# Both weight buffers of a decoder step moved by 64 bytes in the on-chip memory

## The reference

```
proj  = einsum('btnc,ncd->btnd', br, w_branch)
x = x + sum(sigmoid(zg) * proj) @ w_o
h = rmsnorm(x) @ w_up
x = x + square(relu(h)) @ w_down
```

## Time and profile before

| | |
|---|---|
| median of 3 runs | 943.7 us (943.46 to 943.88) |
| profiled execution | 943.61 us, its span 941.8 us |
| TensorE matmuls | 937.0 us busy, 7930 instructions |
| TensorE weight loads | 907.2 us busy, 7930 instructions |
| VectorE | 671.2 us busy |
| ScalarE | 476.8 us busy |
| GpSimd | 40.9 us busy |
| granted TensorE clock | 1.000 of full speed |

### The profile page before, as it was taken

The page is one execution under the profiler, slowest core; times in us unless marked ns, Lnnn a source line. Parts: engine busy times, 40 slices in busy tenths (PEclk is TensorE's granted clock), DMA queues, the critical chain, the costliest instruction groups (busy, mean ns, idle before and its releaser), DMA issues.

```text
span 941.8 us, 18907 instructions
## 1 busy us (share of the span) xinstructions
PE 937.0 (99%) x7930; PEld 907.2 (96%) x7930; DVE 671.2 (71%) x1057; ACT 476.8 (51%) x708; POOL 40.9 (4%) x61
## 2 busy tenths in 40 slices
PE   9999999999999999999999999999999999999998
PEld 8999898999999999999999998999999999999998
DVE  7788788948866765555758787889498676656464
ACT  7439553463654353534653586436537543535261
POOL 0340000000000000000004200000000000000000
PEclk9999999999999999999999999999999999999999
DMA  8756444444454585454557453544444546645542
GB/s 314 261 197 207 151 147 135 136 138 154 157 180 138 198 300 188 159 180 151 174 178 265 167 218 110 168 129 142 136 151 158 169 149 222 202 158 163 187 144 95
DMA packets 44853, 164.26 MB, mean 174 GB/s; under 512 B 5057, under 2 KB 7489, under 8 KB 44225
## 3 DMA queue, kind: packets, MB, share of 16 engines
q1 hardware_dynamic: 43488, 153.03, 48.6%
q0 software_dynamic: 1136, 9.83, 2.7%
q10 hardware_dynamic: 144, 0.20, 0.1%
HBM read 153.30 MB, written 10.29 MB: 174 GB/s over the span
## 4 chain that ended last, share of the span: by engine, by line
PE 98%; DMA 1%; ACT 0%; SPq 0%; DVE 0%; issue 0%; ACTq 0%
PE pz L440 90%; PE pm L440 6%; DMA xp<-in_x_in 1%; PE pm L635 1%; DVE w_lo L1083 0%; ACT w_hi L852 0%; PE pm L698 0%; PE pm L688 0%; SPq L381 0%; SPq L383 0%; ACT rstd L870 0%; ACT w_hi L1031 0%; PE pm L587 0%; ACT a_hi L861 0%; DVE xp L1128 0%
## 5 line engine op out<-in xcount | busy, mean ns | idle before, releaser
L852 ACT ACTIVATE w_hi<-raw 128x1024 fp32r<-128x1024 f32 x265 | 274.1, 1050 | 199.4 <-PE pz L440 194.7
L440 PE MATMUL pz<-a_hi,w_hi 128*128 128x288 f32 x1376 | 370.7, 300 | 0.9 <-ACT w_hi L1031 0.5
L440 PE MATMUL pz<-a_hi,w_lo 128*128 128x288 f32 x1376 | 364.8, 295 | 0.0
L440 PE MATMUL pz<-a_lo,w_hi 128*128 128x288 f32 x1376 | 363.5, 294 | 0.0
L1083 DVE TENSOR_TENSOR w_lo<-raw,w_hi 128x1024 fp32r<-128x1024 f32 x265 | 321.0, 1221 | 37.4 <-ACT w_hi L852 37.3
L440 PEld LDWEIGHTS pz<-a_hi,w_hi 128*128 128x128 f32 x1376 | 244.9, 188 | 11.4 <-issue 7.7
L440 PEld LDWEIGHTS pz<-a_lo,w_hi 128*128 128x128 f32 x1376 | 245.3, 188 | 0.3
L440 PEld LDWEIGHTS pz<-a_hi,w_lo 128*128 128x128 f32 x1376 | 243.6, 188 | 0.2 <-DVE w_lo L1486 0.2
L440 PE MATMUL pz<-h_hi,w_hi 128*128 128x288 f32 x768 | 190.9, 296 | 0.0
L440 PE MATMUL pz<-h_hi,w_lo 128*128 128x288 f32 x768 | 190.4, 295 | 0.0
L440 PE MATMUL pz<-h_lo,w_hi 128*128 128x288 f32 x768 | 189.3, 294 | 0.0
(11 more groups left out here) (174 smaller groups left out, 541.0 us busy)
## 6 DMA issues: line engine op xcount, KB each, us to landing
raw<-in_w SPq DMA_DIRECT2D x265, 512.0 KB, 3.8
arena<-in_s SPq DMA_DIRECT2D x2, 2048.0 KB, 9.3
out_ss_out<-arena POOLq DMA_DIRECT2D x2, 2048.0 KB, 8.0
out_u_out<-arena POOLq DMA_DIRECT2D x2, 864.0 KB, 9.7
arena<-arena SPq DMA_DIRECT2D x8, 180.0 KB, 3.1
arena<-in_kcT SPq DMA_DIRECT2D x2, 512.0 KB, 4.5
arena<-in_vc SPq DMA_DIRECT2D x2, 512.0 KB, 6.0
out_kc_out<-in_kc_kept POOLq DMA_DIRECT2D x1, 992.0 KB, 7.1
```

The lines of the kernel that those rows point to most:

```text
L440: return nc.tensor.matmul(out, a, b, start=start, stop=stop, **kw)
L852: act_fn(w_hi[:, r], raw[:, r], ACT.Copy).then_inc(s["w_hi"], 1)
```

## The change

Two tensors of 16 floats (64 bytes in each partition) are named between others, one ahead of `w_hi` and one behind `w_lo`. Nothing reads or writes them. Each engine runs the same instructions in the same order as before.

```diff
         raw = sb("raw", [P, RING, UW])
+        gap_w = sb("gap_w", [P, 16])
         w_hi = sb("w_hi", [P, RING, UW], F32R)
         w_lo = sb("w_lo", [P, RING, UW], F32R)
+        gap_x = sb("gap_x", [P, 16])
         xp = sb("xp", [P, DEPTH * NPAR + KT * T])
```

## The result

The changed kernel takes 947.99 us (median of 6 runs, 947.85 to 948.61), the kernel before in the same session 944.07: a ratio of 1.0044 with a 95% interval of 1.0035 to 1.0054. It is slower by 4 us, a small loss and clear of noise. I had forecast no change with 0.66, and a loss with 0.17.

The account below looks back on a forecast made before the run. TensorE's step between matmuls was taken as the bound. Loads and matmuls each added 6432 x 0 ns, other engines' costs were covered: 941.8 + 0, with 1.8 us around it 943.6; forecast 943.7 us, range 942 to 945.5.

Parts of the forecast that it names:

- What bounds the kernel: TensorE's row of 6432 matmuls bounds the kernel; each nanosecond in the step between them is worth 6.43 us.
- The price of today's meeting as zero: Matmuls with and without a load beside them take equally long, so the two reads cost each other 0 today.
- 0.29: Nanoseconds of change in the matmul step that would make 0.2% (1.9 us), about what a measurement can tell.
- Changes which half, not how often: Moving the load by 64 bytes leaves both reads in the same 128-byte half about half the time.
- Matmuls: 6432 x 0 ns: Matmul term of the sum: activations still start at 64 past a multiple of 128, so no step changes.
- Weights off a multiple of 128: An odd start does not lengthen a weight load, as with loads from `consts` (188 ns): 6432 x 0 ns.
- The rival in which the load becomes the bound: A load from an odd 64 touches five pieces, 0.137 us against a step of 0.132: 32 us slower, 976; chance 0.07.
- Both operands at the same phase: Weights and activations both at 64; equal-phase pooling matmuls, 121 ns a pass, show no collision, though a weaker test.
- the two reads meet: Rival: load and matmul begin in the same half and activations wait; 71 us slower, a tenth 951 us; chance 0.10.
- the step gets shorter: Rival: equal phases take away the step's 11 ns excess; 71 us faster, 872 us, a tenth 936; chance 0.17.
- the 71 us of the excess: The step's 11 ns above the 121 ns of a pooling pass, over 6432 matmuls.
- ScalarE and VectorE: Splits writing weight halves at 64: 32 ns each (8.5 us) for ScalarE, 7 ns (1.9 us) for VectorE, covered by waits.

Follow-up runs that it names:

- the sweep of four starts: Both weight buffers starting 0, 32, 64 or 96 bytes past a multiple of 128, activations at 64: 943.9 to 944.1, 951.33, 947.99 and 944.61 us.
- The half loads: `a_lo`/`h_lo` matmuls with `w_hi` in units and pairs take 64 of 128 weight columns: 944.55 us at the addresses before the change, 946.63 us at the changed ones.
- exchanged: Against the kernel before, weights start at 64 past a multiple of 128 and activations at 0 (before: 0 and 64): 944.77 us, ratio 1.0007.

## Why the prediction was wrong

- **What bounds the kernel: right.** Each nanosecond of the step is worth 6.43 us, and the whole result is 0.58 to 1 ns of a step of 132.
- **"The price of today's meeting as zero": not shown.** The comparison of a matmul with and without a load beside it sees when a matmul ends, in hundredths of a microsecond. The changed kernel passes the same comparison and is slower. It could not have told 0 from 0.7 ns, and 0.29 was what mattered. I wrote that bound myself and did not hold the test against it.
- **"Changes which half, not how often": wrong, and the step that failed.** It took the meetings of the two reads for an average over a step, which a shift of the load cannot change. The two kernels that move only TensorE's reads show that a shift of 64 bytes costs, and the sweep of four starts that the cost goes with the place. "Matmuls: 6432 x 0 ns" should have been 6432 x 0.7, which is the 4.4 us of the span. An average needs reads that meet by chance, and these start together: in the trace before, 6284 of the 6432 loads start 2 to 5 ns behind a matmul. That this is why the place counts is argued and not shown.
- **Weights off a multiple of 128: right.** The load stayed at 188 ns, and weights at 64 with activations at 0 lose nothing measurable in the time of the whole kernel. The rival in which the load becomes the bound is out. The earlier trace rows were read too freely for it: a matmul starts at 41.68, between the two loads, so that a load alone takes 0.11 us is not shown by them. The half loads bear the figure out: 64 columns less save 53 ns, an estimate of 106 ns for 128.
- **Both operands at the same phase: the nearest row misled.** The pooling matmuls, at equal phases, had no row at other phases beside them, so a loss could not have been seen, and 7 steps read to 0.01 us tell little under 1.4 ns a step. They are also of another type, at nearly twice the time for a column. I had called it the weaker test and still took its answer.
- **The rival "the two reads meet": right in its place, wrong in its form.** It is TensorE's two reads, and I gave it 0.10. But it is not "the first access of each pair": weights at 32 lose more than weights at 64, and a half load leaves it in many single units and nearly removes it in pairs. Its price was 4 us, near a twentieth of the 71 us that I gave as its full size.
- **The rival "the step gets shorter": half of it.** Steps can be won by phase, 1.7 us with `w_lo` alone moved, but not by equal phases and not the 71 us of the excess. The shortest long stretch of all kernels, 161.58 us, still has a step of 132.0 ns. The rule in the Trainium skill, "TensorE: Matmul & The Clock Gate", section "Back-to-back issue gap", gives by an estimate 122.5 ns for an isolated matmul of 288 columns, and none of these kernels met it.
- **ScalarE and VectorE: covered, as forecast, with the sizes exchanged.** From the earlier trace rows I had 32 ns a split for ScalarE and 7 for VectorE; the splits below are 1 ns and 9 ns longer than before. TensorE's waits for the two in the largest group of loads went from 2.4 to 2.5 us, and ScalarE still waits 191.3 us for TensorE (194.7 before).

Groups by form of ScalarE and of VectorE (busy us, mean ns of one, idle before and releasers), the splits of the kernel before, then of the changed one:

```profile
L852 ACT ACTIVATE w_hi<-raw 128x1024 fp32r<-128x1024 f32 x265 | 274.1, 1050 | 199.4 <-PE pz L440 194.7 <-DMA raw<-in_w 4.6
...
L1083 DVE TENSOR_TENSOR w_lo<-raw,w_hi 128x1024 fp32r<-128x1024 f32 x265 | 321.0, 1221 | 37.4 <-ACT w_hi L852 37.3
```

```profile
L854 ACT ACTIVATE w_hi<-raw 128x1024 fp32r<-128x1024 f32 x265 | 274.2, 1051 | 200.8 <-PE pz L442 191.3 <-DMA raw<-in_w 9.4
...
L1085 DVE TENSOR_TENSOR w_lo<-raw,w_hi 128x1024 fp32r<-128x1024 f32 x265 | 323.3, 1230 | 38.1 <-ACT w_hi L854 38.1
```

Open is the rule by which addresses make the step. What is shown is that it is TensorE's own two reads, that a shift of both together by 64 or 128 bytes changes the time little (948.0 against 947.8 us, 944.8 and 943.9 against 944.0), and that the order of reads has a part in it. Phases modulo 128 do not fix the step alone: one layout had two steps in one execution.

## What to carry to other kernels

Where a loop of matmuls is the bound and each matmul loads its own weights, the place of weights and activations in the on-chip memory is a parameter of the step, worth up to 0.8% here, and no row of the profile names it. It is cheap to sweep by a gap of some bytes, and best read from long undisturbed stretches, where a tenth of a nanosecond in a step is visible, and from more than one of them. A test that finds "no effect" says something only if its grain is finer than the effect that would count.

## What the runs showed that was not expected

- Moving `w_lo` alone by 64 bytes beats both kernels: 942.26 us against 944.0 before, 0.9981 (0.9972 to 0.9990).
- Differences of 32 and 96 bytes are not mirror images: 944.61 and 951.33 us.
- Loads of half the length (135 ns against 188) leave the step of pairs where it was, 162.18 against 162.10 us for 1224.
- The same addresses in another order of chunks cost 1.8 us.
- Two stretches of the same kind of work in one execution can take different steps: exchanged, 132.5 and 132.9 ns.
